# A two-layer hybrid attention trunk on one core: another order for VectorE's chain, held weight splits and early output tiles in the differential stage

## The reference

```python
def differential_attention(q, k, v, lam):
    ...
        s = jnp.einsum('bhcqd,bhckd->bhcqk', qblk.astype(jnp.float32), kf) * scale
        ...
        p = jax.nn.softmax(jnp.where(causal, s, -jnp.inf), axis=-1)
        a = p[:, :, 0] - lam * p[:, :, 1]
        return jnp.einsum('bhqk,bhke->bhqe', a, vf)

def diff_layer(x, k, v, norm_g, w_in, q_norm_g, lam_params, subln_g, w_out, layer_idx, cos, sin):
    h = rms_norm(x, norm_g)
    q, gate = jnp.split(h @ w_in, 2, axis=-1)
    ...
    q = apply_rope(rms_norm(q, q_norm_g), cos[:, :, None, None, :], sin[:, :, None, None, :])
    ...
    o = differential_attention(q, k, v, lam)
    o = rms_norm(o, subln_g) * (1.0 - lam_init)
    o = o.transpose(0, 2, 1, 3).reshape(B, S, D_MODEL).astype(x.dtype)
    return (jax.nn.silu(gate) * o) @ w_out
```

## Time and profile before

| | |
|---|---|
| median of 3 runs | 695.98 us (693.69 to 698.03) |
| the profiled execution's own time | 692.85 us |
| its span, first to last instruction | 691.6 us |
| mean granted TensorE clock | 0.975 of full speed |
| PE busy | 646.1 us (93%) |
| DVE / ACT / POOL busy | 433.1 / 328.6 / 343.8 us |

### The profile page before, as it was taken

The page is one execution under the profiler, slowest core; times in us unless marked ns, Lnnn a source line. Parts: engine busy times, 40 slices in busy tenths (PEclk is TensorE's granted clock), DMA queues, the critical chain, the costliest instruction groups (busy, mean ns, idle before and its releaser), DMA issues.

```text
span 691.6 us, 10026 instructions
## 1 busy us (share of the span) xinstructions
PE 646.1 (93%) x3388; PEld 544.9 (79%) x3388; DVE 433.1 (63%) x685; ACT 328.6 (48%) x712; POOL 343.8 (50%) x325
## 2 busy tenths in 40 slices
PE   4999989999999999899989999997899889687998
PEld 4788778888888888788878888886787777576886
DVE  3493295775957758473073788048888899777321
ACT  4342466475664756633255454224564356535220
POOL 5564675544555442445324544485744465253241
PEclk9999999999999999999999999999999999878999
DMA  7432231221212210021112222223222111210141
GB/s 243 119 91 77 67 102 46 62 61 45 61 45 61 61 45 30 16 77 62 65 58 88 95 85 83 84 76 99 78 65 57 34 42 46 87 51 26 50 138 61
DMA packets 61774, 49.08 MB, mean 71 GB/s; under 512 B 7729, under 2 KB 48817, under 8 KB 61745
## 3 DMA queue, kind: packets, MB, share of 16 engines
q1 hardware_dynamic: 58064, 48.25, 22.6%
q10 hardware_dynamic: 3680, 0.46, 0.4%
HBM read 44.50 MB, written 2.10 MB: 67 GB/s over the span
## 4 chain that ended last, share of the span: by engine, by line
PE 72%; DVE 16%; issue 5%; ACT 3%; POOL 2%; DMA 1%; DVEq 0%; SPq 0%; POOLq 0%; ACTq 0%
PE bank L560 19%; PE bank L561 19%; PE bank L562 19%; PE bank L673 6%; DVE small L1585 3%; PE bank L658 2%; DVE ge L1340 1%; DVE pr L1608 1%; PE bank L821 1%; POOL w_lo L470 1%; PE bank L841 1%; DVE v L1308 1%; DVE hi L1384 1%; DMA xs<-in_x 1%; PE bank L637 1%
## 5 line engine op out<-in xcount | busy, mean ns | idle before, releaser
L470 POOL TENSOR_TENSOR w_lo<-w_raw,w_hi 128x512 fp32r<-128x512 f32 x100 | 139.6, 1396 | 8.0
L458 POOL TENSOR_TENSOR w_lo<-w_raw,w_hi 128x512 fp32r<-128x512 f32 x60 | 81.1, 1354 | 122.0 <-ACT w_hi L954 121.6
L468 POOL CAST w_hi<-w_raw 128x512 fp32r<-128x512 f32 x100 | 72.3, 723 | 123.1 <-PE bank L562 74.2
L560 PE MATMUL bank<-h_hi,w_hi 128*128 128x512 f32 x320 | 130.8, 409 | 2.6 <-ACT q L1152 2.6
L560 PE MATMUL bank<-w_hi,h_hi 128*128 128x512 f32 x320 | 127.6, 399 | 4.0 <-DVE h_lo L1314 2.9
L561 PE MATMUL bank<-h_lo,w_hi 128*128 128x512 f32 x320 | 127.1, 397 | 0.0
L562 PE MATMUL bank<-h_hi,w_lo 128*128 128x512 f32 x320 | 126.7, 396 | 0.0
L562 PE MATMUL bank<-w_hi,h_lo 128*128 128x512 f32 x320 | 125.2, 391 | 0.0
L561 PE MATMUL bank<-w_lo,h_hi 128*128 128x512 f32 x320 | 125.1, 391 | 0.0
L560 PEld LDWEIGHTS bank<-h_hi,w_hi 128*128 128x128 f32 x320 | 61.8, 193 | 15.9 <-ACT q L1152 3.0
L954 ACT ACTIVATE w_hi<-w_raw 128x512 fp32r<-128x512 f32 x60 | 37.6, 628 | 77.0 <-PE bank L562 77.0
(11 more groups left out here) (176 smaller groups left out, 1229.7 us busy)
## 6 DMA issues: line engine op xcount, KB each, us to landing
w_raw<-in_a_w_in SPq DMA_DIRECT2D x64, 256.0 KB, 2.8
w_raw<-in_w_kv SPq DMA_DIRECT2D x32, 256.0 KB, 3.1
w_raw<-in_b_w_in SPq DMA_DIRECT2D x32, 256.0 KB, 2.8
w_raw<-in_a_w_out SPq DMA_DIRECT2D x16, 256.0 KB, 2.7
w_raw<-in_b_w_out SPq DMA_DIRECT2D x16, 256.0 KB, 2.8
xs<-in_x SPq DMA_DIRECT2D x4, 512.0 KB, 5.3
qrot<-qs SPq DMA_DIRECT2D x32, 64.0 KB, 2.0
out_x<-xs SPq DMA_DIRECT2D x8, 256.0 KB, 2.6
```

What stands on the lines that cost most here:

```text
L458: nc.gpsimd.tensor_tensor(w_lo[s][:, :], w_raw[s][:, :], w_hi[s][:, :].bitcast(F32), ALU.subtract).then_inc(s_w, 1)
L468: nc.gpsimd.tensor_copy(w_hi[s][:, :], w_raw[s][:, :]).then_inc(s_whi, 1)
L470: nc.gpsimd.tensor_tensor(w_lo[s][:, :], w_raw[s][:, :], w_hi[s][:, :].bitcast(F32), ALU.subtract).then_inc(s_w, 1)
L560: pe.matmul(o, ahi, bhi, start=start, stop=False, skip_group_check=True)
```

## The change

- DVE: in a head, `o_scale` moves ahead of `gate_log`; `q_add` moves behind the first `combine`; the second `combine` comes before `o_times_gate` and `q_low`. The silu of the gate gets a semaphore of its own (`s_si`), which ACT (to overwrite the gate's buffers) and `o_times_gate` wait for.
- ACT: `q_round` moves behind the exponentials and `q_copy`.
- POOL: the slab splits of a head wait, from head 1 on, for `s_cm` of that head.
- PE: the masks of component 1 come first, without a wait; those of component 0 wait bank by bank. Head 6 projects its gate before attention times V and the last gate behind it. The output projection is cut: four row tiles of its first four slabs (`early_tile`) run between the pieces of head 7, into banks chosen by `OUT_BANK_B`.
- SP: the last gate's two slabs load ahead of the last q swap.

```diff
@@ SP
         block_slabs(H_GATES, win_b, D + 6 * P)
+        block_slabs(H_GATES + 2, win_b, D + 7 * P)
         swap_halves(8)
-        block_slabs(H_GATES + 2, win_b, D + 7 * P)
@@ POOL, in the loop; the same for heads 5 and 6 below it
             key(i + 1)
+            pool.wait_ge(s_cm, i + 1)
             split(H_BODY + 4, i, 4)
...
@@ PE scores_b
-            if not first:
-                pe.wait_ge(s_al, h * 3 + 48)
-            for b in range(3):
-                for c in (0, 1):
+            for c in (1, 0):
+                for b in range(3):
+                    if c == 0 and not first:
+                        pe.wait_ge(s_al, h * 3 + (46 + b))
                     mask(bank[BANK_B[c, b]][:, :], ...)
@@ PE, from head 6
+        def early_tile(t):
+            for k in range(RING_B):
+                pe.wait_ge(s_o, KT + k + 1)
+                bulk_step(H_OUT + k, 0, k, h2_hi, h2_lo, banks_of=OUT_BANK_B, tiles=(t,))
...
-        late_head(KT - 2, H_GATES, KT - 1)
-        late_head(KT - 1, H_GATES + 2)
+        h = KT - 2
+        scores_b(h, False)
...
+        project(H_GATES, h1_hi, h1_lo, bank[6][:, :], between=lambda: o_roots(h - 2))
+        attend_before(h, 2)
+        sums(h + 1, h - 1)
+        pe.wait_ge(s_gc, h + KT + 1)
+        pe.wait_ge(s_ga, h + KT + 1)
+        project(H_GATES + 2, h1_hi, h1_lo, bank[6][:, :], between=lambda: turn_probs(h))
+        scores_b(KT - 1, False)
         pe.wait_ge(s_gc, 2 * KT)
         pe.wait_ge(s_ga, 2 * KT)
-        attend_b(KT - 1, 3 * KT, bank[6])
+        early_tile(0)
+        o_roots(KT - 3)
+        attend_before(KT - 1, 2)
+        pe.wait_ge(s_pe, 8 * KT - 6)
+        early_tile(1)
+        sums(o=KT - 2)
+        turn_probs(KT - 1)
+        early_tile(2)
+        attend_b(KT - 1, 3 * KT, bank[0])
         o_roots(KT - 2)
+        early_tile(3)
+        bulk_step(H_OUT + 4, 0, 4, h2_hi, h2_lo, banks_of=OUT_BANK_B)
...
@@ ACT head
+            if later is not None and h == KT - 2:
+                gate_parts(h, later)
+            if q_next:
+                act.wait_ge(s_z, h * 6 + 54)
+                q_round(h + 1)
             if not first:
                 output_square(h - 1)
@@ DVE head
-            if q_next:
-                q_add(h + 2)
-            if n_before:
-                gate_log(h + KT)
             if n_before == 2:
                 o_scale(h - 2)
+            if gate:
+                gate_log(h + KT)
...
             combine((3, 2), 2, 4)
+            if q_next:
+                q_add(h + 2)
+            if gate:
+                gate_silu(h + KT)
+            combine((0, 1), 0, 8).then_inc(s_cm, 1)
             if n_before:
-                gate_silu(h + KT)
+                o_times_gate(h - 1)
             if q_next:
                 q_low(h + 2)
-            if n_before:
-                o_times_gate(h - 1)
-            combine((0, 1), 0, 8).then_inc(s_cm, 1)
```

More of the change, by code:

```diff
@@ L541, in _ @@
         key(KT - 2)
+        pool.wait_ge(s_cm, KT - 2)
         split(H_GATES)
@@ L547, in _ @@
         key(KT - 1)
-        value(KT - 2)
+        pool.wait_ge(s_cm, KT - 1)
         split(H_OUT)
         split(H_OUT + 1)
+        value(KT - 2)
+        split(H_OUT + 2)
+        split(H_OUT + 3)
         value(KT - 1)
-        for g in range(H_OUT + 2, N_ALL):
+        for g in range(H_OUT + RING_B, N_ALL):
             split(g)
@@ L911, in _ @@
             head(i, 2)
-        late_head(KT - 2, H_GATES, KT - 1)
-        late_head(KT - 1, H_GATES + 2)
+        h = KT - 2
+        scores_b(h, False)
+        pe.wait_ge(s_gc, h + KT)
+        pe.wait_ge(s_ga, h + KT)
+        project(H_GATES, h1_hi, h1_lo, bank[6][:, :], between=lambda: o_roots(h - 2))
[5 more added lines that the diff above has]
+        scores_b(KT - 1, False)
         pe.wait_ge(s_gc, 2 * KT)
         pe.wait_ge(s_ga, 2 * KT)
-        attend_b(KT - 1, 3 * KT, bank[6])
-        o_roots(KT - 2)
[L919 to L926, removed]
+        early_tile(0)
[7 more added lines that the diff above has]
+        attend_b(KT - 1, 3 * KT, bank[0])
+        o_roots(KT - 2)
+        early_tile(3)
+        bulk_step(H_OUT + 4, 0, 4, h2_hi, h2_lo, banks_of=OUT_BANK_B)
+        pe.wait_ge(s_og, 2 * KT - 1)
+        sums(o=KT - 1)
+        pe.wait_ge(s_o, 2 * KT - 2)
+        bulk_step(H_OUT + 5, 0, 5, h2_hi, h2_lo, banks_of=OUT_BANK_B)
+        o_roots(KT - 1)
+        for k in (KT - 2, KT - 1):
+            pe.wait_ge(s_o, KT + k + 1)
+            bulk_step(H_OUT + k, 0, k, h2_hi, h2_lo, banks_of=OUT_BANK_B)
+        for k in range(KT):
+            bulk_step(H_OUT + KT + k, TT, k, h2_hi, h2_lo, banks_of=OUT_BANK_B)
     @block.scalar
@@ L1224, in gate_parts, with head @@
             gate_log(h + (KT + 1))
-        def head(h, first=False, gate=None, q_used=None, q_next=True):
-            if not first:
+        def head(h, first=False, gate=None, q_used=None, q_next=True, later=None):
+            if gate is not None:
                 gate_parts(h - 1, gate)
+            elif later is not None and h == KT - 1:
+                gate_parts(h, later)
             for b, strips in enumerate(((3,), (2, 0), (1,))):
@@ L1238, in head @@
                     q_square(h + 2)
-                if b == 1:
-                    if q_next:
[L1241 to L1244, removed]
+                if b == 1 and gate is not None:
+                    gate_exp(h + KT)
             if q_used is not None:
                 q_copy(h + 3, q_used)
+            if later is not None and h == KT - 2:
+                gate_parts(h, later)
+            if q_next:
+                act.wait_ge(s_z, h * 6 + 54)
+                q_round(h + 1)
             if not first:
                 output_square(h - 1)
+            if later is not None and h == KT - 1:
+                gate_exp(h + KT + 1)
             c0, c1 = mean_cols(first, not q_next)
@@ L1263, in _ @@
             head(i, gate=i * 4 + H_BODY, q_used=i * 4 + (H_BODY + 2))
[L1264 to L1268, removed]
+        head(KT - 2, gate=H_GATES, later=H_GATES + 2)
+        head(KT - 1, q_next=False, later=H_GATES + 4)
+        output_square(KT - 1, bank[0])
         slab_hi(H_OUT + 4)
@@ L1571, in o_times_gate, with head @@
             dve.wait_ge(s_oq, h + 1)
+            dve.wait_ge(s_si, h + (KT + 1))
             STT(out=ot[:, :], in0=o[:, :], scalar=gsub, op0=ALU.mult, in1=silu[:, :],
                 op1=ALU.mult).then_inc(s_ot, 1)
-        def head(h, n_before, q_next=True, q_after=True):
+        def head(h, n_before, q_next=True, q_after=True, gate=True):
             def biases(v, b):
@@ L1622, in head @@
                 keep_lo(h - 2, h + (KT - 1))
+            if not gate and n_before:
+                gate_log(2 * KT)
+                gate_silu(2 * KT)
             c0, c1 = mean_cols(not n_before, not q_next)
@@ L1642, in _ @@
         q_rotate(2)
-        head(0, 0)
+        head(0, 0, gate=False)
         head(1, 1)
         with dve.Fori(2, KT - 2) as i:
-            st.enter(i, 2, 11)
+            st.enter(i, 2, 10)
             head(i, 2)
@@ L1649, in _ @@
         head(KT - 2, 2, q_after=False)
-        head(KT - 1, 2, q_next=False, q_after=False)
+        gate_log(2 * KT - 1)
+        gate_silu(2 * KT - 1)
+        head(KT - 1, 2, q_next=False, q_after=False, gate=False)
         o_scale(KT - 2)
[L1652 to L1655, removed]
+        keep_hi(KT - 2, 2 * KT - 1)
+        o_times_gate(KT - 1, bank[0])
+        keep_lo(KT - 2, 2 * KT - 1)
         dve.wait_ge(s_sum, KT + 2)
```

23 lines of the change are left out of this document (7 added, 16 removed).

## The result

The changed kernel takes 674.72 us (median of 4 runs, 672.46 to 675.95) against 696.81 (693.69 to 698.03) for the kernel before on the same chip: ratio 0.9679, 95% interval 0.9644 to 0.9713. The forecast was 688.5 us, with a range of 679 to 698. The profiled execution ran 672.46 us with a span of 671.2, against 692.85 and 691.6: 20.4 us less, where 7.5 were forecast.

The account below looks back on a forecast made before the run. PE was taken to set the length, standing still where DVE's chain ends last. Heads 2 to 5 -0.8, head 1 +0.4 and head 6 to the end -7.15 made -7.5 us: median 688.5 us, range 679 to 698.

Parts of the forecast that it names:

- What bounds the kernel: Whole kernel: PE sets the length, standing still where DVE's chain ends last; its clock is full almost everywhere except near the end.
- Heads 1 to 5, what goes: Steady heads (2 to 5): PE's waits of 0.68 us ahead of attention times V and 1.17 ahead of `sums` go.
- Heads 1 to 5, what takes its place: POOL's moved work slows DVE behind `s_cm`: heads 2 to 5 take 22.7 us against 22.9, head 1 21.3.
- seven operations: DVE's SBUF-only steps behind `s_cm`: `q_low`, `keep_hi`, `keep_lo`, three Newton steps, epsilon sums; they take turns with POOL.
- The new wait of 2.8 us at the masks: Steady heads: PE, ready at 17.9 us, waits about 2.8 us at the component-0 masks for `at_lo`.
- The masks by bank: Steady heads: running component 1's masks early gives back 0.35 us.
- Head 6 to the end: First mask of head 6 to last matmul: 73.9 us work, 6.8 new waits, 3.5 clock; 84.2 us, a gain of 7.15.
- the slab split: Output projection: the fifth slab is split only once tile 3 has used the first; PE waits 0.85 us (0 to 2).
- the work that I let stay at 73.9: Head 6 to the end: pure work without waits and clock loss, 73.9 us, unchanged because the matmuls are the same.
- Cleaner heads: Rival, chance 0.25: small DVE operations slip past POOL, heads 1 to 5 take 20.5 to 21 us, median 679.
- The slower rival: Chance 0.10: all seven DVE operations wait for a POOL subtraction or cast; heads of 26.3 us, median 702.4 or 706.
- What the profile would show: Signs: no steady `og` or `ot` waits, 2 to 3.5 us at the masks, 3 to 5 idle ahead of head 6's `sums`.

Follow-up runs that it names:

- e7: The changed kernel with one more wait on PE: in heads 2 to 5 `sums` wait for the kept output's rounding on DVE; 684.33 us.
- e6: The changed kernel with the masks in the old order, all behind the last `at_lo`; 673.39 us, ratio 0.9706.
- e1: The changed kernel without the three waits that hold POOL's slab splits until the second combination; 712.46 us, ratio 1.0278.
- e2: The kernel before with only POOL's hold added, in the loop of heads and ahead of `H_GATES`; 683.87 us, ratio 0.9856.
- e8: The changed kernel with POOL held until `o_times_gate`, one operation later, in the loop and ahead of `H_GATES`; 676.34 us, ratio 0.9719.
- e4: The changed kernel with POOL's V split ahead of the two slab splits behind the hold; 674.48 us, ratio 0.9723.

## Why the prediction was wrong, step by step

- **What bounds the kernel.** Right on the waits, incomplete on the clock. "PE's granted clock is full almost everywhere except near the end" was read from the page's tenths, where a stretch of 3.4 us in a slice of 17 is rounded away. The three stretches in heads 2 to 5 cost 3.4 us by the head that had none and 5.1 by half of their length. That they come with the waits for `ot` ahead of `sums` is what e7 shows.
- **Heads 1 to 5, what goes.** Right: 0.68 and 1.17 went. The combination ends 9.97 us after the first maximum (forecast 9.8).
- **Heads 1 to 5, what takes its place.** This step failed: "9.7 to 10.3 us from `s_cm` to the first `at_lo`" is 6.1. I let seven operations pay for four subtractions and three or four casts. Two subtractions and three casts passed: two operations met casts, one pair slipped into a pause, and the roots on ACT covered part of a subtraction. The new wait of 2.8 us at the masks never came. Four heads of 22.7 were 90.8; they are 78.9. The forecast less that wait was 19.9 a head, and 19.7 was measured. Head 1, forecast at 21.3, is 19.3 for the same reason. Together 14.2 us were gained where 0.4 were forecast. These 13.8 are more than the whole error in the gain (20.4 for 7.5, 12.9); the late part fell short by 1.0.
- **The masks by bank.** The 0.35 is not there: component 1's masks do run early, but PE then waits 0.27 for the copy of q (e6).
- **Head 6 to the end.** Forecast 7.15, measured 6.1 from head 6's first maximum on. In the forecast's own stretch, from the first mask (582.14) to the last matmul's end (668.32), it is 86.2 us for 84.2 forecast and 91.35 before: a gain of 5.2. The waits were to sum to 6.8 and do (4.97 + 0.78 + 1.04 = 6.79), with a larger one for `ot` (4.97 for 4.0, as the silu ended 11.5 us after the first mask and not 10.4: the mask now stands 2.7 us ahead of the first maximum, before 1.8), none for the last gate's copy (1.2 forecast), and in place of the slab split (0.85) one for the last kept output. The clock cost 4.3 (half of 8.60 busy us) where I took 3.5. The last 1.1 is in the work that I let stay at 73.9: 86.2 less waits and clock is 75.0. No run shows why the same number of matmuls took longer.
- **Rivals.** "Cleaner heads" was the right mechanism, at 0.25. Its price was wrong: 20.5 to 21 a head, above the 19.9 that the forecast's own sum gives without the wait, so 679 was its centre and the range stopped there. The slower rival, all seven operations behind a subtraction or cast, did not come. Waiting itself is seen (`h_hi`, and two Newton steps that end with POOL's running instruction), but for the small steps only its remainder was left, 0.50 and 0.52 us, and two others slipped through. What makes this change slower is something else, the order without the hold (e1, 2.8% slower than before).
- **What the profile would show.** Right: no wait on `og` or `ot` in heads 2 to 5, idle time ahead of head 6's `sums` released by `ot`, waits under 2 us later. Wrong: the wait at the masks, and PE dense from the fifth slab on: 1.04 for `h_lo` stands at 643.51, eleven us behind that slab's start.

Not settled: whether the clock falls by the length of the wait or by its place. Waits of 1.0 to 1.17 ahead of `sums` had a half-clock stretch behind them in six of eight cases, and the 1.73 in head 1 of the kernel before had none; waits of 0.7 at the masks (e2) and of 0.27 did not. No kernel here put 1.1 us at the masks in every head. What a half-clock stretch costs is open too: 1.1 us in the kernel before, 0.1 to 0.2 in e7, where DVE's chain is as late without it, and 1.7 by half of its 3.4. Nor was it tried to shorten DVE's chain and PE's work together, which by e8 is what a head under 19.7 would need.

## What to carry to other kernels

Where two engines slow each other on shared ports, sum up what each operation costs ahead of the one that the bottleneck waits for and behind it: a hold that only moves the slow part behind that point was worth 1.4% alone, and the order made for it lost 2.8% without it. When estimating turns, lay the two timelines side by side operation by operation; a product of count and turn was too high by 4 us in every head here. And list the stretches at half clock by their times before summing waits: a short wait ahead of very small matmuls may carry a second cost in the work behind it. Price that cost against a head without such a stretch, and not by half of its length, since a wait behind it may take its place.

## What the runs showed that I had not expected

- A wait of 1.0 to 1.1 us of PE ahead of `sums` is followed by 3.4 to 6.8 us at a granted clock of 0.50, in which the work is dense (e7, in three of four heads). In the kernel before, five waits of 1.17 to 1.73 stood there in heads 1 to 5, and three stretches followed.
- Small DVE operations slip into POOL's pause of 0.19 us between the cast and the subtraction of a V split, at 0.17 and 0.16 us, two in a row; the same epsilon sums took 1.26 where a slab's subtraction followed its cast without that pause (e4).
- POOL started 0.35 us after the combination's end (535.36 to 535.71), in the middle of `ot`. `ot`, which reads a bank, took 0.74 there, and 0.74 in e8 too, where POOL was idle until it had ended (538.26 to 539.00, POOL's cast at 539.35).
